# Latent attention: order of the query and key jobs between the score tiles, and the rope keys' split moved into the Fourier phase

## Chip, cores and metric

One NeuronCore of one Trainium2 chip runs the whole program. The metric is the device time of one execution in microseconds; the kernel before takes 3359.33 us (median of 3 runs, 3356.55 to 3360.12).

## The reference, cut to what matters

The program is a chain of two transformer blocks. The change lies in the first, which has two layers. Each layer projects 1040 tokens, mixes them by a Fourier transform, by average pooling and by a latent attention of four heads, gates and joins the three and multiplies by an output matrix. The attention is

```
def mla_mix(c_q, c_kv, k_r, q_norm_w, w_uq, kv_norm_w, w_ukv, cos, sin):
    dq = QK_NOPE_DIM + QK_ROPE_DIM                      # 128 + 64
    q = (rms_norm(c_q, q_norm_w) @ w_uq).reshape(B, L, MLA_HEADS, dq)
    q = concat([q[..., :QK_NOPE_DIM], apply_rope(q[..., QK_NOPE_DIM:], cos, sin)])
    kv = (rms_norm(c_kv, kv_norm_w) @ w_ukv).reshape(B, L, MLA_HEADS, QK_NOPE_DIM + V_HEAD_DIM)
    k_nope, v = kv[..., :QK_NOPE_DIM], kv[..., QK_NOPE_DIM:]
    k_rope = apply_rope(k_r, cos, sin)                  # one for all heads
    k = concat([k_nope, broadcast(k_rope)])
    s = einsum('bqhd,bkhd->bhqk', q, k) * dq ** -0.5
    return einsum('bhqk,bkhd->bqhd', softmax(s), v)
```

## The kernel before

All engines run one static program; `core.phase` opens a block with its own semaphores, and every engine passes from one block to the next. In each of the two layers the blocks are the input products, the Fourier and pool phase (`fourier_and_pool`, L864), and the heads together with the output product (`latent_heads`, L1068, inside `gemm`, L217).

**Precision.** Products that count run as sums of a high and a low part: a value x becomes x_hi (ACT, copied to the rounded type fp32r) and x_lo = x - x_hi (DVE). The projections of queries, keys and values (L1160, L1167) run in plain fp32, two matmul records for each 128-deep step.

**Fourier phase.** PE multiplies by a 64-point table (L909), then by the time tables (L922), each of the two channel halves j into four PSUM banks, then by the head matrices (L897). ACT evicts (L936, L942), DVE forms the spectrum from the evicted even part (L968, L972) and gates (L977). Between the pooling and the first spectrum, DVE applies the rotation to the keys (L957, L958, L960), for which it waits for the rope table, the last of the phase's DMAs (L891). PE's head product of half j waits for four DVE instructions of that half (L929).

**Heads.** The 1040 queries, padded to 1044, are 9 tiles of 116 rows (NH = 9, HT = 116), the keys and the query chunks 3 chunks of 348 columns (CH1). With four heads there are 36 score tiles, called steps s = 9n + i here: head n, step i. In step s PE does, in this order: `score(s)`, 15 matmuls into banks 0 to 2 (L1139); the jobs of the step (L1187); and nine transposes of the probabilities of step s - 1 into banks 3 to 5 (L1176). The next scores reuse banks 0 to 2 and wait for the exponential of step s (`exp_done`, L1130), and at i = 0, 3, 6 also for the query chunk i // 3 (L1128), at i = 0 for the head's keys (L1126). DVE takes in step s, in order: the row maximum (L1248) and its scaling (L1250), the rotation of a rope job (L1256, L1257, L1259), the reciprocal (L1262) and the normalisation (L1264), the low parts of the step's jobs (L1282) or the gated output of a value product (L1270), and the low part of the transposed tile s - 1 (L1293). ACT takes the exponential (L1201), the high parts of the jobs (L1211 to L1217) and of the transposed tile (L1234).

**Jobs.** `head_jobs` (L1040) is an order written by hand. There are five kinds: kn (a chunk of keys, 4 matmul records), qn and qr (a chunk of queries without and with rope, 6 records each), v (four tiles of values, 8 products) and pv (27 matmuls, probabilities times values for three tiles). All use PSUM banks 6 and 7 in turn: job j waits until job j - 2 is saved (L1147). pv also waits for the low part of its last transposed tile (L1151). Query chunks lie in two slots in turn (`slot_of`). The order before:

```
1044	    jobs = {0: [("qr", n, 1), ("qn", n, 1)], 1: [("pv", n - 1, 2)], 2: [("v", n, 0), ("v", n, 1)],
1045	            3: [("v", n, 2), ("qn", n, 2)], 4: [("pv", n, 0)], 5: [("qr", n, 2), ("kn", n + 1, 0)],
1046	            6: [("kn", n + 1, 1), ("kn", n + 1, 2)], 7: [("pv", n, 1)], 8: [("qr", n + 1, 0), ("qn", n + 1, 0)]}
```

Steps -4 to -1 hold only the jobs that step numbers of a head -1 would have; jobs of heads outside 0 to 3 fall away. SP loads the weights of heads 2 and 3 when the last query job of head n - 2 is done (L1115).

**Rope keys.** At the start of the heads ACT rounds the rotated keys twice, into both halves of `kr_hi` (L1195), and DVE forms `kr_lo` (L1241) and zeroes its second half (L1242). The first scores wait for it (L1123). While this goes on, POOL splits a weight tile of the output product (L199, L203).

**End.** In steps 33, 34, 36 and 37 ACT and DVE also split rows of the mixed result for the output product (`first_tile`, L324 and L330), whose first matmuls (L212) follow the last scores' exponential.

Of the kernel before, what the change touches and what calls it, by code (L numbers as in the profile page):

```python
# [822 lines left out]
def first_block(core, io, h, ident, ones):  # L823
# [6 lines left out]
    for layer in range(LAYERS):  # L830
        with core.scope():
# [4 lines left out]
            with core.scope():  # L836
# [11 lines left out]
                with core.scope():  # L848
                    fourier_and_pool(core, io, layer, slots, mix, r, vecs)
            with core.scope():  # L850
                heads = partial(latent_heads, core, io, layer, slots, mix, r, wqk, ident, HeadTensors(core))
# [12 lines left out]
def fourier_and_pool(core, io, layer, slots, mix, rope, vecs):  # L864
# [13 lines left out]
    first = (0, L1 - QT * NQ)  # L878

    with core.phase("z_done", "z_saved", *[f"tab{t}" for t in range(NQ)], "time_done", "even_saved", "spectrum_ready",  # L880
                    "pool_done", "pool_saved", "head_done", "rope_parts", "rope_in") as (block, *sems):
# [3 lines left out]
         rope_in) = sems[2 + NQ:]  # L885
# [46 lines left out]
        @block.scalar  # L932
        def _(act):
            for t in range(NQ):
                act.wait_ge(z_done, t + 1)
                nc.scalar.activation(z[:, t].rearrange("p j a n -> p (j a n)"), core.psum[0:QT, t % 2, :],  # L936
                                     ACT.Copy).then_inc(z_saved, 1)
            for j in range(2):
                act.wait_ge(time_done, j + 1)
                even = evens[:, j, :]  # L940
                for half in range(2):
                    nc.scalar.activation(even[:, half * HA:half * HA + widths[half]],  # L942
                                         core.psum[:, 4 * j + half, 0:widths[half]],
                                         ACT.Copy).then_inc(even_saved, 1)

        @block.vector
        def _(dve):
# [12 lines left out]
            nc.vector.tensor_tensor(kr, kr, krs, ALU.add)  # L960
# [79 lines left out]
def head_jobs(s):  # L1040


    n, i = divmod(s, NH)
    jobs = {0: [("qr", n, 1), ("qn", n, 1)], 1: [("pv", n - 1, 2)], 2: [("v", n, 0), ("v", n, 1)],
            3: [("v", n, 2), ("qn", n, 2)], 4: [("pv", n, 0)], 5: [("qr", n, 2), ("kn", n + 1, 0)],
            6: [("kn", n + 1, 1), ("kn", n + 1, 2)], 7: [("pv", n, 1)], 8: [("qr", n + 1, 0), ("qn", n + 1, 0)]}
    return [job for job in jobs[i] if 0 <= job[1] < MLA_HEADS]


class HeadTensors:  # L1050
# [3 lines left out]
    def __init__(self, core):  # L1054
        kn0 = core.sb("kn_hi", [P, TP], FR, 32), core.sb("kn_lo", [P, TP], FR, 32)
        self.kr_hi, self.kr_lo = core.sb("kr_hi", [P, TP], FR, 32), core.sb("kr_lo", [P, TP], FR, 32)
# [8 lines left out]
        self.qa, self.qb = (core.sb(name, [64, CH1], align=32) for name in ("rope_cos", "rope_sin"))  # L1065


def latent_heads(core, io, layer, slots, mix, rope, wqk, ident, tensors, first_tile):  # L1068
# [6 lines left out]
    steps = range(-4, tiles + 2)  # L1075
# [8 lines left out]
    kr = slots[0:64, KR, :]  # L1084
# [19 lines left out]
    with core.phase("kr_hi_done", "kr_lo_done", "pads_set", "wqk_in2", "wqk_in3", "job_done", "job_hi", "job_saved", "qr_step",  # L1104
                    "qr_ready", "scores_done", "max_ready", "bias_ready", "exp_done", "inv_done", "prob_ready",
                    "turned_done", "turned_hi", "turned_saved") as \
            (block, kr_hi_done, kr_lo_done, pads_set, wqk_in2, wqk_in3, job_done, job_hi, job_saved, qr_step, qr_ready,
# [5 lines left out]
        def _(sp):  # L1113
            for n in (2, 3):
                sp.wait_ge(job_done, number["qr", n - 2, 2] + 1)  # L1115
# [3 lines left out]
        def _(pe):  # L1119
            def score(s):  # L1120
                n, i = divmod(s, NH)
                if s == 0:
                    pe.wait_ge(kr_lo_done, 2)  # L1123
# [69 lines left out]
        def _(act):  # L1193
            for half in range(2):
                nc.scalar.activation(kr_hi[64 * half:64 * half + 64], kr, ACT.Copy).then_inc(kr_hi_done, 1)  # L1195
# [3002 lines left out]
```

## Time and profile before

| | |
|---|---|
| median of 3 runs | 3359.33 us (3356.55 to 3360.12) |
| the profiled execution, its own time | 3359.92 us |
| its span | 3358.1 us |
| PE busy | 3196.7 us, 95% |
| weight loads (PEld) busy | 2726.0 us, 81% |
| DVE busy | 2058.2 us, 61% |
| ACT busy | 1010.1 us, 30% |
| POOL busy | 938.9 us, 28% |

One slice of the page's 40 is 84 us; the heads of layer 0 are in slices 4 to 7, those of layer 1 in slices 11 to 14. PE shows 8 or 9 tenths busy in each. The time of the profiled execution is 1.8 us above its span, the part before and after the first and last instruction. In a timeline row the duration of a merged group of matmuls includes the modelled tail of its last; the distance to the start of the next group is the time that PE gave to it.

### The profile page before, as it was taken

Reading aid. Unit: us, or ns where it says so; the run is one execution under the profiler, and the core shown is the slowest. Engines: PE = TensorE matmul, PEld = TensorE weight load, DVE = VectorE, ACT = ScalarE, POOL = GpSimd, SP = SyncE. Lnnn points to the kernel's source line nnn. Section 1 sums busy time; section 2 is a strip of 40 time slices with the busy share of each in tenths; the row PEclk is TensorE's granted clock in tenths of the full one; section 3 lists DMA queues with packets and bytes.
Section 4 is the critical chain, followed back from the end, with each engine's and each line's share of the span. In section 5 each row is a group of like instructions: output and inputs, shape, how many; then the busy total and the mean of one; then the engine's idle time right before and its main releaser. Section 6 shows DMA issues by size and latency. Waiting matters only on the chain. (4 is left out here: it accounts for less than half of the span.)

```text
span 3358.1 us, 41800 instructions
## 1 busy us (share of the span) xinstructions
PE 3196.7 (95%) x17082; PEld 2726.0 (81%) x17082; DVE 2058.2 (61%) x2422; ACT 1010.1 (30%) x1456; POOL 938.9 (28%) x617
## 2 busy tenths in 40 slices
PE   8998999999899999999998999999999999999997
PEld 7997888999788898878867996666777787888875
DVE  5535664444466634556456554655676766897788
ACT  2113332101233320000022221555432644344643
POOL 3320001233000032333224322100142443555575
PEclk9999999999999999999999999999999999999998
DMA  3120000211100013323331003211361454455443
GB/s 135 45 65 9 21 1 20 77 45 45 33 21 8 1 45 135 130 93 97 103 126 54 1 1 111 72 42 38 117 227 59 146 172 156 132 183 171 147 158 119
DMA packets 111758, 282.12 MB, mean 84 GB/s; under 512 B 15010, under 2 KB 20770, under 8 KB 111552
## 3 DMA queue, kind: packets, MB, share of 16 engines
q1 hardware_dynamic: 107104, 263.19, 23.4%
q10 hardware_dynamic: 4464, 16.25, 1.2%
q8 instruction: 136, 2.23, 0.3%
q14 instruction: 54, 0.44, 0.0%
HBM read 237.37 MB, written 41.42 MB: 83 GB/s over the span
## 5 line engine op out<-in xcount | busy, mean ns | idle before, releaser
L3639 PE MATMUL psum<-x,w_hi 128*128 128x512 f32 x2016 | 627.0, 392 | 8.3 <-DVE x L3610 3.1
L199 POOL CAST w_hi<-w_raw 128x1024 fp32r<-128x1024 f32 x116 | 126.2, 1088 | 1795.9 <-PE psum L212 1112.0
L3639 PEld LDWEIGHTS psum<-x,w_hi 128*128 128x128 f32 x2016 | 379.1, 189 | 93.1 <-issue 6.9
L3639 PE MATMUL psum<-x,w_lo 128*128 128x512 f32 x1008 | 393.4, 390 | 0.0
L3524 POOL TENSOR_TENSOR w_lo<-w_sum,w_hi 128x512 fp32r<-128x512 f32 x180 | 252.9, 1412 | 330.0 <-ACT w_hi L3518 330.0
L727 PE MATMUL psum<-h,w_hi 128*128 128x512 f32 x1024 | 328.1, 402 | 15.2 <-PEq L126 11.5
L203 POOL TENSOR_TENSOR w_lo<-w_raw,w_hi 128x1024 fp32r<-128x1024 f32 x116 | 301.9, 2602 | 16.4 <-DVE y L1533 7.2
L727 PEld LDWEIGHTS psum<-h,w_hi 128*128 128x128 f32 x1024 | 190.2, 192 | 63.1 <-issue 21.9
L3639 PEld LDWEIGHTS psum<-x,w_lo 128*128 128x128 f32 x1008 | 190.0, 189 | 39.8
L212 PE MATMUL psum<-hn_hi,w_hi 128*128 128x348 f32 x864 | 188.9, 327 | 16.5 <-DVE hn_lo L409 15.1
L727 PE MATMUL psum<-h,w_lo 128*128 128x512 f32 x512 | 202.7, 396 | 0.0
L212 PE MATMUL psum<-h,w_hi 128*128 128x512 f32 x736 | 197.1, 389 | 0.0
L212 PE MATMUL psum<-hn_lo,w_hi 128*128 128x348 f32 x864 | 185.2, 323 | 0.0
L212 PE MATMUL psum<-hn_hi,w_lo 128*128 128x348 f32 x864 | 184.9, 322 | 0.0
L3518 ACT ACTIVATE w_hi<-w_sum 128x512 fp32r<-128x512 f32 x180 | 112.3, 630 | 208.2 <-DVE w_sum L3506 208.1
L212 PEld LDWEIGHTS psum<-hn_hi,w_hi 128*128 128x128 f32 x864 | 146.7, 189 | 20.2 <-issue 12.7
L212 PEld LDWEIGHTS psum<-h,w_hi 128*128 128x128 f32 x736 | 138.1, 188 | 28.7 <-issue 0.2
L1201 ACT ACTIVATE prob<-psum,softmax_small 116x1044 f32<-116x1044 f32 x72 | 81.5, 1132 | 227.2 <-DVE softmax_small L1250 227.2
L212 PEld LDWEIGHTS psum<-hn_lo,w_hi 128*128 128x128 f32 x864 | 147.2, 190 | 0.0
L212 PEld LDWEIGHTS psum<-hn_hi,w_lo 128*128 128x128 f32 x864 | 146.6, 189 | 0.0
L3506 DVE TENSOR_TENSOR w_sum<-w_raw 128x512 f32<-128x512 f32 x121 | 119.8, 993 | 28.5 <-PE psum L3639 22.2
L1167 PE MATMUL psum<-kept_slots,wqk 128*128 128x348 f32 x384 | 122.4, 466 | 11.0 <-DVE kn_lo L1282 7.8
(464 smaller groups left out, 6491.4 us busy)
## 6 DMA issues: line engine op xcount, KB each, us to landing
w_raw<-in_w_mlp SPq DMA_DIRECT2D x169, 256.0 KB, 2.9
norm_factor<-in_w_mlp SPq DMA_DIRECT2D x87, 256.0 KB, 2.8
w_raw<-in_w_mlp SPq DMA_DIRECT2D x42, 512.0 KB, 3.4
w_raw<-in_w_in SPq DMA_DIRECT2D x36, 512.0 KB, 3.4
w_raw<-in_w_gates SPq DMA_DIRECT2D x32, 512.0 KB, 4.2
gates_kept<-gate_stage SPq DMA_DIRECT2D x64, 256.0 KB, 2.1
gates<-gates_kept SPq DMA_DIRECT2D x32, 512.0 KB, 3.3
w_raw<-in_w_out SPq DMA_DIRECT2D x24, 512.0 KB, 3.5
```

Of the source, the lines that this page charges most:

```text
L199: self.core.nc.gpsimd.tensor_copy(self.hi[:, g % 2], self.raw[:, g % 2]).then_inc(self.hi_done, 1)
L203: self.core.nc.gpsimd.tensor_tensor(self.lo[:, g % 2], self.raw[:, g % 2], self.hi[:, g % 2].bitcast(F32), ALU.subtract) \
L212: last = nc.tensor.matmul(acc[:, c, :], w[:, g % 2, k, :], x(k)[:, c * ch:(c + 1) * ch], start=(k == 0 and part == 0), stop=(k == kt - 1 a ...
L727: last = nc.tensor.matmul(self.core.psum[:, self.bank(x // KT), :], one[:, g % 2, k, :], other(k)[:, c * CH2:(c + 1) * CH2], start=(k == 0 ...
L1167: last = nc.tensor.matmul(bank(j), wqk[n % 2][:, k0 + k, cols], slots[:, src + k, chunk(c)], start=(k == 0), stop=(k == kt - 1))
L1201: nc.scalar.activation(prob[s % 2].rearrange("p (c n) -> p c n", c=3), scores, ACT.Exp, bias=nmx[:, s % 2:s % 2 + 1], scale=MLA_SCALE, acc ...
L3506: self.core.nc.vector.tensor_tensor(self.slot(self.core.weights.sums, j), raw[:, 0:4], raw[:, 4:8], self.SUMS[q]).then_inc(self.w_summed, 1)
L3518: self.core.nc.scalar.activation(self.slot(self.core.weights.hi, j), self.weight_source(j), ACT.Copy) \
L3524: self.core.nc.gpsimd.tensor_tensor(self.slot(w.lo, j), self.weight_source(j), self.slot(w.hi, j).bitcast(F32), ALU.subtract).then_inc(sel ...
L3639: last = self.core.nc.tensor.matmul(out, one[:, k, :], other[:, k, :], start=(group == 0 and k == 0 and part == 0), stop=(group == second ...
```

## The change

The order of jobs is rewritten, so that a query chunk is made at least one step before the scores that need it; steps begin at -9 instead of -4, so that the jobs of a head -1 all run ahead. The split of the rope keys moves out of the heads into the Fourier phase, into which the heads' tensors are passed; for that, the heads' memory is laid out first and `kr_hi` and `kr_lo` stand at its end, beyond what the Fourier phase uses. The wait for head weights goes by qn instead of qr.

```diff
-                with core.scope():
-                    fourier_and_pool(core, io, layer, slots, mix, r, vecs)
             with core.scope():
-                heads = partial(latent_heads, core, io, layer, slots, mix, r, wqk, ident, HeadTensors(core))
+                tensors = HeadTensors(core)
+                heads = partial(latent_heads, core, io, layer, slots, mix, r, wqk, ident, tensors)
+            with core.scope():
+                core.sb("early_slots", [P, CKV + A_GATE - F_GATE, TP])
+                fourier_and_pool(core, io, layer, slots, mix, r, vecs, tensors)
...
         def _(act):
...
+            act.wait_ge(kr_ready, 1)
+            for half in range(2):
+                nc.scalar.activation(kr_hi[64 * half:64 * half + 64], slots[0:64, KR, :], ACT.Copy) \
+                    .then_inc(kr_hi_done, 1)
             for j in range(2):
                 act.wait_ge(time_done, j + 1)
...
-            nc.vector.tensor_tensor(kr, kr, krs, ALU.add)
+            nc.vector.tensor_tensor(kr, kr, krs, ALU.add).then_inc(kr_ready, 1)
+            dve.wait_ge(kr_ready, 1)
+            dve.wait_ge(kr_hi_done, 2)
+            nc.vector.tensor_tensor(kr_lo[0:64], kr, kr_hi[0:64].bitcast(F32), ALU.subtract)
+            nc.vector.tensor_tensor(kr_lo[64:P], kr_hi[64:P].bitcast(F32), kr_hi[64:P].bitcast(F32), ALU.subtract)
...
-    jobs = {0: [("qr", n, 1), ("qn", n, 1)], 1: [("pv", n - 1, 2)], 2: [("v", n, 0), ("v", n, 1)],
-            3: [("v", n, 2), ("qn", n, 2)], 4: [("pv", n, 0)], 5: [("qr", n, 2), ("kn", n + 1, 0)],
-            6: [("kn", n + 1, 1), ("kn", n + 1, 2)], 7: [("pv", n, 1)], 8: [("qr", n + 1, 0), ("qn", n + 1, 0)]}
+    jobs = {0: [("kn", n + 1, 0), ("kn", n + 1, 1)], 1: [("pv", n - 1, 2)], 2: [("v", n, 0), ("v", n, 1)],
+            3: [("v", n, 2), ("qr", n, 2)], 4: [("qn", n, 2), ("pv", n, 0)], 5: [("qr", n + 1, 0)],
+            6: [("qn", n + 1, 0)], 7: [("kn", n + 1, 2), ("pv", n, 1)], 8: [("qr", n + 1, 1), ("qn", n + 1, 1)]}
...
-    steps = range(-4, tiles + 2)
+    steps = range(-NH, tiles + 2)
...
-                sp.wait_ge(job_done, number["qr", n - 2, 2] + 1)
+                sp.wait_ge(job_done, number["qn", n - 2, 2] + 1)
...
-                    pe.wait_ge(kr_lo_done, 2)
...
-            for half in range(2):
-                nc.scalar.activation(kr_hi[64 * half:64 * half + 64], kr, ACT.Copy).then_inc(kr_hi_done, 1)
...
-            dve.wait_ge(kr_hi_done, 2)
-            nc.vector.tensor_tensor(kr_lo[0:64], kr, kr_hi[0:64].bitcast(F32), ALU.subtract).then_inc(kr_lo_done, 1)
-            nc.vector.tensor_tensor(kr_lo[64:P], kr_hi[64:P].bitcast(F32), kr_hi[64:P].bitcast(F32), ALU.subtract) \
-                .then_inc(kr_lo_done, 1)
```

## Rows read from the trace of the kernel before

**Rows 1.** Waits of PE, 235:545: engine, line, output, releaser: us in total, times, longest

```profile
PE psum L1139 <- DVE qr_both L1282: 5.4, 4, 2.2
PE psum L1139 <- DVE qn_lo L1282: 4.9, 4, 1.7
```

**Rows 2.** Timeline, start of layer 0's heads: start us, us, engine, line, operation

```profile
268.39 2.58 PE L1167 MATMUL psum<-kept_slots,wqk 128*128 128x348 f32 x8 [1.59 <-PEq L126]
...
269.55 2.35 POOL L203 TENSOR_TENSOR w_lo<-w_raw,w_hi 128x1024 fp32r<-128x1024 f32 x1
270.57 0.91 ACT L1215 ACTIVATE kn_hi<-psum 128x348 fp32r<-128x348 f32 x2
270.57 2.42 DVE L1241 TENSOR_TENSOR kr_lo<-kept_slots,kr_hi 64x1044 fp32r<-64x1044 f32 x1 [2.08 <-ACT kr_hi L1195]
...
274.87 6.56 PE L1167 MATMUL psum<-kept_slots,wqk 128*128 128x348 f32 x16 [3.90 <-DVE kn_lo L1282]
...
283.17 0.70 PE L1139 MATMUL psum<-kn_hi,qn_hi 128*116 128x348 f32 x3 [1.73 <-DVE qn_lo L1282]
```

**Rows 3.** Timeline of PE, head 1: scores' first group, value product, transposes

```profile
345.43 0.71 PE L1139 MATMUL psum<-kn_hi,qn_hi 128*116 128x348 f32 x3 [1.07 <-DVE qn_lo L1282]
...
354.90 0.40 PE L1155 MATMUL psum<-pT_hi,v_hi 116*128 116x348 f32 x1
...
359.26 1.05 PE L1176 MATMUL psum<-ident,prob 116*116 116x116 f32 x9
360.08 0.70 PE L1139 MATMUL psum<-kn_hi,qn_hi 128*116 128x348 f32 x3
...
372.29 0.70 PE L1139 MATMUL psum<-kn_hi,qn_hi 128*116 128x348 f32 x3
...
409.43 0.70 PE L1139 MATMUL psum<-kn_hi,qn_hi 128*116 128x348 f32 x3 [1.07 <-DVE qn_lo L1282]
```

**Rows 4.** Timeline of DVE and PE, head 0, step 1 to step 2

```profile
291.70 1.25 DVE L1248 TENSOR_REDUCE softmax_small<-psum 116x1 f32<-116x1044 f32 x1 [0.56 <-PE psum L1139]
...
294.44 0.73 PE L1139 MATMUL psum<-kn_hi,qn_hi 128*116 128x348 f32 x3 [1.88 <-ACT prob L1201]
```

**Rows 5.** Timeline, head 3, step 5 (one rope job) to step 6

```profile
508.31 0.70 PE L1139 MATMUL psum<-kn_hi,qn_hi 128*116 128x348 f32 x3
...
510.75 1.92 PE L1167 MATMUL psum<-kept_slots,wqk 128*128 128x348 f32 x6
...
512.51 1.06 PE L1176 MATMUL psum<-ident,prob 116*116 116x116 f32 x9
512.71 0.51 DVE L1256 TENSOR_TENSOR rope_cos<-psum,norm_factor 64x348 f32<-64x348 f32 x1 [0.32 <-PE psum L1167]
...
515.79 0.72 PE L1139 MATMUL psum<-kn_hi,qn_hi 128*116 128x348 f32 x3 [2.23 <-DVE qr_both L1282]
515.86 1.25 DVE L1293 TENSOR_TENSOR pT_lo<-psum,pT_hi 116x1044 fp32r<-116x1044 f32 x1
```

**Rows 6.** Timeline, head 3, steps 6 and 7 and the end

```profile
519.45 1.25 DVE L1248 TENSOR_REDUCE softmax_small<-psum 116x1 f32<-116x1044 f32 x1 [2.34 <-PE psum L1139]
...
526.79 0.40 PE L1155 MATMUL psum<-pT_hi,v_hi 116*128 116x348 f32 x1 [1.98 <-issue]
...
532.69 1.05 PE L1176 MATMUL psum<-ident,prob 116*116 116x116 f32 x9
...
539.53 0.75 PE L212 MATMUL psum<-mix_hi,w_hi 128*128 128x348 f32 x3 [1.43 <-ACT prob L1201]
```

**Rows 7.** Windows of 1 us: length, PE, PEld, DVE, ACT, POOL, then PEclk, DMA

```profile
296.00:297.00 1.00, 1.00 (x5) 1.00 (x4) 0.60 (x1) 0.00 (x0) 0.00 (x0) 0.50 0.00 0
...
528.00:529.00 1.00, 1.00 (x5) 1.00 (x4) 0.03 (x1) 0.93 (x1) 0.00 (x0) 0.50 0.00 0
```

**Rows 8.** Timeline, Fourier phase of layer 0

```profile
250.93 1.24 DVE L960 TENSOR_TENSOR kept_slots<-kept_slots,mix 64x1044 f32<-64x1044 f32 x1
...
262.40 1.92 PE L897 MATMUL psum<-early_slots,last 128*128 128x348 f32 x6
```

More of the change, by code:

```diff
@@ L861, in first_block, with fourier_and_pool @@
     return vecs, r[:], comes_first
-def fourier_and_pool(core, io, layer, slots, mix, rope, vecs):
+def fourier_and_pool(core, io, layer, slots, mix, rope, vecs, tensors):
     nc = core.nc
@@ L878, in fourier_and_pool @@
     first = (0, L1 - QT * NQ)
+    kr_hi, kr_lo = tensors.kr_hi, tensors.kr_lo
     with core.phase("z_done", "z_saved", *[f"tab{t}" for t in range(NQ)], "time_done", "even_saved", "spectrum_ready",
-                    "pool_done", "pool_saved", "head_done", "rope_parts", "rope_in") as (block, *sems):
+                    "pool_done", "pool_saved", "head_done", "rope_parts", "rope_in", "kr_ready",
+                    "kr_hi_done") as (block, *sems):
         z_done, z_saved = sems[0:2]
@@ L884, in fourier_and_pool @@
         (time_done, even_saved, spectrum_ready, pool_done, pool_saved, head_done, rope_parts,
-         rope_in) = sems[2 + NQ:]
+         rope_in, kr_ready, kr_hi_done) = sems[2 + NQ:]
         @block.sync
@@ L1055, in __init__ @@
         kn0 = core.sb("kn_hi", [P, TP], FR, 32), core.sb("kn_lo", [P, TP], FR, 32)
-        self.kr_hi, self.kr_lo = core.sb("kr_hi", [P, TP], FR, 32), core.sb("kr_lo", [P, TP], FR, 32)
         kn1 = core.sb("kn_hi", [P, TP], FR, 32), core.sb("kn_lo", [P, TP], FR, 32)
@@ L1065, in __init__ @@
         self.qa, self.qb = (core.sb(name, [64, CH1], align=32) for name in ("rope_cos", "rope_sin"))
+        self.kr_hi, self.kr_lo = core.sb("kr_hi", [P, TP], FR, 32), core.sb("kr_lo", [P, TP], FR, 32)
 def latent_heads(core, io, layer, slots, mix, rope, wqk, ident, tensors, first_tile):
@@ L1083, in latent_heads @@
     small, prob, kn_hi, kn_lo, kr_hi, kr_lo, qa, qb = t.small, t.prob, t.kn_hi, t.kn_lo, t.kr_hi, t.kr_lo, t.qa, t.qb
-    kr = slots[0:64, KR, :]
     scores = core.psum[0:HT, 0:3, 0:CH1]
@@ L1103, in v_bank @@
         return core.psum[0:HT, 6 + j % 2, 0:n * P].rearrange("p (t n) -> p t n", t=n)
-    with core.phase("kr_hi_done", "kr_lo_done", "pads_set", "wqk_in2", "wqk_in3", "job_done", "job_hi", "job_saved", "qr_step",
+    with core.phase("pads_set", "wqk_in2", "wqk_in3", "job_done", "job_hi", "job_saved", "qr_step",
                     "qr_ready", "scores_done", "max_ready", "bias_ready", "exp_done", "inv_done", "prob_ready",
                     "turned_done", "turned_hi", "turned_saved") as \
-            (block, kr_hi_done, kr_lo_done, pads_set, wqk_in2, wqk_in3, job_done, job_hi, job_saved, qr_step, qr_ready,
+            (block, pads_set, wqk_in2, wqk_in3, job_done, job_hi, job_saved, qr_step, qr_ready,
              scores_done, max_ready, bias_ready, exp_done, inv_done, prob_ready, turned_done, turned_hi,
```

## The prediction

> **What bounds the kernel now.** I read the page first: PE is busy in 95% of the span (the table above), no other engine above 61%. So the change can gain only PE's idle time and time at the lower clock. Then the waits of PE over the heads of layer 0. Two of them are for a query chunk made one step before it is used, 5.4 and 4.9 us, four times each [rows 1]. Then the timeline of PE with its distances from start to start, and around each wait the other engines. Layer 1 repeats layer 0, so I work out one layer and double it.
>
> **Prices on PE**, all start to start. Scores 2.44, from 508.31 to 510.75; a q job 1.76 [rows 5]. Transposes 0.82; pv 4.36 [rows 3], of which I keep 4.30 where another job stands before it. A kn is 1.17: the row of eight records is 2.58 long with a tail of 0.24 [rows 2]. A step is thus 3.26 plus its jobs. But the next scores also wait for the exponential. DVE starts 0.20 after PE hands over (the rope multiply at 512.71 after the job that ends at 512.51 [rows 5]), and from the start of the maximum to the next scores it is 2.74 (291.70 to 294.44 [rows 4]). So no step is under 2.44 + 0.20 + 2.74 = 5.38.
>
> **The start.** Now: two kn, then PE stands 3.90, since the rope keys' low part, 2.42 on DVE, is ahead of kn's on DVE; then sixteen records take 6.56, and scores begin at 283.17, 14.78 after 268.39 [rows 2]. After: kn0 is out at 269.6; its rounding (half of the 0.91 for two [rows 2]) and its low part (0.5, as the rope multiply of the same 348 columns [rows 5]), with handovers, let qr0 start at 270.9; qn0 follows. kn2 must wait until qr0 is saved. The multiply starts 1.96 after its job's start, at 272.9, and in head 3 the scores waited for the same saving until 3.08 after the multiply [rows 5]; here the reciprocal and scaling are not between, so I take 2.9. kn2 starts at 275.8, after a stall of 1.3, and with kn2, qr1 and qn1 (4.69) scores start at 280.45. Gain 2.7, with two more q jobs already done. Their 3.5 us come back as shorter later steps.
>
> **Head 0.** Step 0: two kn, 2.44 + 2.34 is under the floor: 5.38. Step 1: no job, 5.38. Steps 2 and 3 keep their jobs' sum; they take 12.21 in head 1 [rows 3]. In head 0 the clock falls in step 2, after the stall of 1.88 [rows 4]: the granted clock of one of its stretches is 0.50, 1.2 instead of 2.4 GHz [rows 7]. I count 1.6 for it before and after. Step 4: qn and pv, 2.44 + 1.76 + 4.30 + 0.82 = 9.32. Step 5: one qr, 3.26 + 1.76 = 5.02, so the floor holds, 5.38.
>
> Step 6 is where the change gives something back. In a step with a lone qr, DVE's last low part starts 3.15 after the multiply and takes 1.25 [rows 5], so it ends 4.40 + 3.15 + 1.25 = 8.80 after the step's scores began. The next scores began at 5.38 and their maximum could start at 8.02; it starts at 8.84. Step 6 lasts 8.84 + 2.74 - 5.38 = 6.20, against 5.02 of work. Step 7: kn and pv, 8.73. Step 8: two q jobs, 6.78, without today's wait of 1.07. Steps 4 to 8 give 36.41. Head 0 is 5.38 + 5.38 + 12.21 + 1.6 + 36.41 = 60.98, before 62.26 (283.17 to 345.43): **1.3 gained**.
>
> **Heads 1 and 2.** Before 64.00 (345.43 to 409.43), and nearly the same in head 2. Now steps 4 to 8 take 37.14 (372.29 to 409.43), steps 0 and 1 14.65 (345.43 to 360.08) [rows 3]. After: step 0 is 3.26 + 2.34 = 5.60. The pv of step 1 waits for DVE's last instruction of step 0, which two kn low parts make later: 2.64 + 2.74 + 0.9 (reciprocal and scaling, an estimate: under the 1.25 of a low part of equal length) + 1.05 (two low parts of a chunk) + 1.25 = 8.6 after step 0 began, 0.65 after pv could start; today it is 0.25. Step 1: 3.26 + 4.36 + 0.65 = 8.27. The sum is 13.87 + 12.21 + 36.41 = 62.49: **1.5 gained in each**. In step 3 the qr moves behind v and its saving is late, so step 4's maximum is some 1.3 late; pv covers that.
>
> **Head 3.** No head follows, so steps 0, 5, 6 and 8 have no jobs. After: 5.38; 3.26 + 4.36 = 7.62; 12.21; 9.32; 5.38; then step 6 starts. In it DVE and ACT also split rows for the output product, and pv of step 7 starts 7.34 after step 6's maximum (519.45 to 526.79). That keeps, so pv starts 2.64 + 7.34 = 9.98 after step 6 began. pv 4.36, and from the transposes behind it to the output product 6.84 (532.69 to 539.53) [rows 6]. Sum 61.1. Before: 539.53 - 473.4 = 66.1, with 473.4 as 409.43 + 64.0. **5.0 gained**, half of it the lower clock before, in step 6 and in the pv (526.79 to 532.69 is 5.90 for 4.36 [rows 6]; a stretch in it was granted 0.50 [rows 7]).
>
> **The clock.** Before, three of the stalls of 1.88 or more were followed by the lower clock: 1.88 [rows 4], 2.23 [rows 5], the one of 1.98 before the pv [rows 6]; that of 1.06 to 1.07 (row 409.43) was not. After, head 3 has empty steps 0, 5 and 6, each with a stall of 2.1, and one of 2.2 before the last pv but one. If each lowers the clock, 1.6 + 1.0 + 1.5 come back (one falls inside the wait of pv). The shortest of them is at the edge of what the rows show, so I take 2.7 of 4.1. Ends: 0 and 4.1.
>
> **The Fourier phase.** The key rotation ends at 252.2. ACT rounds twice, 2.2, until 254.4, and evicts even part 0 some 0.7 later than now; DVE then runs both low parts, 2.42 + 1.24 at most, until 258.1, and four spectrum instructions, until 259.5. PE does not need them before 262.40 [rows 8]. I count zero; the cover is 2.9 of time products. Without it the price would be at most those 2.2 + 3.7 = 5.9 a layer. The 2.42 is long because POOL runs a subtract from 269.55 to 271.90 while DVE, of the same length otherwise as the 1.24 of the rotation [rows 8], begins at 270.57 [rows 2]: DVE starts its work only when POOL is done. The Trainium skill, page "SBUF — State Buffer", section "SBUF: two separate sides", has the rule: a DVE instruction with two SBUF inputs and a GpSimd instruction that reads SBUF exclude each other, each for its whole length. By it the low part would take 1.24 in the Fourier phase, where POOL is idle, and the cover would be 4.1; the sum stays.
>
> **SP, memory.** The weights of heads 2 and 3 are asked for one step earlier and needed four steps earlier, still over four steps after the request. Addresses change for the heads' tensors only; no row prices that, zero, between -1 and +1 a layer.
>
> **Sum per layer:** 2.7 + 1.3 + 3.0 + 5.0 - 2.7 = 9.3; two layers 18.6. The profiled execution took 3359.9, 0.6 above the median: 3341.3 in its terms, 3340.7 against the median. I say 3341.
>
> **Rivals.**
> **A, lower clock nearly gone** (12%): none of head 3's stalls lowers it, and head 0's step 2 keeps the full clock too. 12.0 + 1.6 a layer: 3332. For it: none of the stalls below 1.1 did so. Against: that of 1.88 did.
> **B, the heads become DVE's** (8%): the late maxima of steps 4, 6 and 1 don't heal, since DVE starts each next step late. Then each head loses some 2 more, 8 a layer, and about 1 a layer is left: 3357, no change. Against it: after every pv DVE has over 4 us to catch up.
> **C, slower by the clock** (3%): every stall over a microsecond, some twelve a layer, costs one lowering of 1.5, 18 a layer. It decides from eight on: 12.0 - 18 is 6 a layer lost, 3371. Against it: the stalls of 1.06 and 1.07 in the rows, followed by full speed.
> **D, the rope split on the path** (4%): head products wait for the spectrum, up to 5.9 a layer, 3.4 are left: 3353, no change that can be told. Against it: the cover of 2.9.
> My own case: 73%.
>
> **Range.** 3332 to 3349: the low end is A, the high end all of head 3's lowered clocks and 0.07 us of error on each of 72 steps. About 0.2%, 6.7 us, is what a measurement of this kernel can tell from no change. Faster by more: my case and A, 0.85; within: B and D, 0.12; slower: C, 0.03.
>
> **What would show it.** PE's waits for qr_both and qn_lo in scores gone; in their place waits for the exponential, about 0.4 in step 5 and 1.2 in step 6 of heads 0 to 2 and 2.1 in the empty steps of head 3. First scores 12.1 after the heads' first matmul. No wait of PE in the Fourier phase beyond today's; the rope low part at 1.24 there. A longer distance from step 6 to step 7, or waits of pv over 0.7, would make B right; PEclk under 1 in heads 1 and 2, C. The step that I trust least is the clock in head 3.

## The result, and the profile after

| | before | after |
|---|---|---|
| median | 3358.01 us (3356.55 to 3360.12, 4 runs) | 3337.27 us (3336.07 to 3342.22, 4 runs) |
| profiled execution | 3359.92 us | 3342.22 us |
| its span | 3358.1 us | 3340.4 us |

Both kernels ran side by side on one chip. The ratio is 0.994 with a 95% interval of 0.9924 to 0.9955: 20.7 us less. The forecast was 3341, so 3.7 too high, and inside its range.

From the page of the changed kernel (busy us of each engine, share of the span, instructions):

```profile
PE 3194.2 (96%) x17082; PEld 2724.5 (82%) x17082; DVE 2054.5 (62%) x2422; ACT 1010.0 (30%) x1456; POOL 939.5 (28%) x617
```

PE does the same work in 17.7 us less span. The waits of PE in the heads of layer 0 (line, releaser: us in total, times, longest), to be held against [rows 1]:

```profile
PE psum L1149 <- ACT prob L1209: 10.3, 11, 1.9
...
PE psum L1165 <- issue: 2.4, 3, 2.0
...
PE psum L1177 <- DVE qr_both L1286: 1.1, 1, 1.1
...
PE psum L901 <- DVE early_slots L984: 0.5, 1, 0.5
```

The scores (now L1149) no longer wait for a query chunk. They wait for the exponential only. The start of the heads, in the timeline of all engines (start, us, engine, line), the rows that answer to [rows 2, 4 and 8]:

```profile
253.34 1.24 DVE L971 TENSOR_TENSOR kr_lo<-kept_slots,kr_hi 64x1044 fp32r<-64x1044 f32 x1 [2.31 <-ACT kr_hi L944]
...
258.56 0.42 DVE L984 TENSOR_TENSOR early_slots<-even_part,psum 128x259 f32<-128x259 f32 x1
...
265.46 1.92 PE L901 MATMUL psum<-early_slots,last 128*128 128x348 f32 x6
...
271.46 6.29 PE L1177 MATMUL psum<-kept_slots,wqk 128*128 128x348 f32 x20 [1.59 <-PEq L126]
...
276.03 0.51 DVE L1260 TENSOR_TENSOR rope_cos<-psum,norm_factor 64x348 f32<-64x348 f32 x1 [0.94 <-PE psum L1177]
...
278.84 4.95 PE L1177 MATMUL psum<-kept_slots,wqk 128*128 128x348 f32 x16 [1.09 <-DVE qr_both L1286]
...
283.36 0.90 PE L1149 MATMUL psum<-kn_hi,qn_hi 128*116 128x348 f32 x3
...
294.35 0.73 PE L1149 MATMUL psum<-kn_hi,qn_hi 128*116 128x348 f32 x3 [1.88 <-ACT prob L1209]
```

The rope keys' low part is made at 253.34, in 1.24 us instead of 2.42. Twenty records of the first jobs run on end, and the scores start at 283.36, 11.90 after 271.46. Head 1, steps 6 and 7, DVE and PE, to be held against [rows 5]:

```profile
383.56 0.70 PE L1149 MATMUL psum<-kn_hi,qn_hi 128*116 128x348 f32 x3 [0.22 <-ACT prob L1209]
...
385.64 1.25 DVE L1297 TENSOR_TENSOR pT_lo<-psum,pT_hi 116x1044 fp32r<-116x1044 f32 x1
...
386.80 1.24 DVE L1252 TENSOR_REDUCE softmax_small<-psum 116x1 f32<-116x1044 f32 x1
...
389.54 0.72 PE L1149 MATMUL psum<-kn_hi,qn_hi 128*116 128x348 f32 x3 [0.73 <-ACT prob L1209]
...
398.29 0.71 PE L1149 MATMUL psum<-kn_hi,qn_hi 128*116 128x348 f32 x3
```

The maximum at 386.80 stands behind the low part at 385.64, and step 6 lasts 5.98. Head 3, the scores of steps 6 and 7, the value product, and the output product (answers to [rows 6]):

```profile
507.28 0.70 PE L1149 MATMUL psum<-kn_hi,qn_hi 128*116 128x348 f32 x3 [1.65 <-ACT prob L1209]
...
512.66 0.73 PE L1149 MATMUL psum<-kn_hi,qn_hi 128*116 128x348 f32 x3 [1.89 <-ACT prob L1209]
...
517.26 0.40 PE L1165 MATMUL psum<-pT_hi,v_hi 116*128 116x348 f32 x1 [1.98 <-issue]
...
523.16 1.05 PE L1186 MATMUL psum<-ident,prob 116*116 116x116 f32 x9
...
529.99 0.74 PE L212 MATMUL psum<-mix_hi,w_hi 128*128 128x348 f32 x3 [1.43 <-ACT prob L1209]
```

The value product from 517.26 to 523.16 takes 5.90 for 4.36. It is a lowered stretch, a piece of PE's work at the lower clock: a microsecond of it (length, PE, PEld, DVE, ACT, POOL, PEclk, DMA, GB/s) was granted half the clock, 1.2 instead of 2.4 GHz, as one before in [rows 7]:

```profile
519.00:520.00 1.00, 1.00 (x5) 1.00 (x5) 0.18 (x2) 1.00 (x3) 0.00 (x0) 0.50 0.00 0
```

Step by step, from one scores' start to the next, in layer 0:

| us | forecast | measured |
|---|---|---|
| first matmul of the heads to first scores | 12.06 | 11.90 |
| head 0, step 0; step 1 | 5.38; 5.38 | 5.57; 5.42 |
| head 0, steps 2 and 3 | 12.21 + 1.6 | 12.26, at the full clock |
| heads 1 and 2, steps 0 and 1 | 13.87 | 13.63 (head 1) |
| steps 2 and 3 of head 1 | 12.21 | 12.22 |
| step 4 of head 1 | 9.32 | 9.32 |
| step 5; step 6 | 5.38; 6.20 | 5.47; 5.98 |
| step 7; step 8 | 8.73; 6.78 | 8.75; 6.78 |
| head 0; 1; 2 | 60.98; 62.49; 62.49 | 59.56; 62.15; 62.21 |
| head 3 | 61.1, and 2.7 of clock | 62.71, of which 1.54 clock |

Layer 1 gives the same lengths within 0.03, but for two: step 2 of its head 0 takes 8.35 instead of 6.80, at the lower clock, and its head 3 keeps the full clock. **Where the time came from:** from the heads' first matmul to the output product's first it was 271.14 and 271.15 us in the two layers, and is 258.53 and 258.60. That is 25.2 less. Part of it is clock. Before, each layer had four lowered stretches in its heads: the sixteen records behind the stall of 3.90 [rows 2], which take 6.56 where sixteen take 4.95 at 278.84 after the change, step 2 of head 0 (8.34 for 6.80), and steps 6 and 7 of head 3 (6.40 and 11.32, for 5.42 and 9.80 in the split-only kernel below). The window around the first of them, before:

```profile
275.00:281.00 6.00, 6.00 (x16) 3.74 (x16) 1.98 (x5) 0.46 (x1) 0.00 (x0) 0.74 0.00 0
```

Together the four cost 5.7 a layer and the one left after costs 1.5, so about 4.1 of the 12.6 a layer is the lower clock, and the rest is waits. The span is 17.7 shorter, so 7.5 went elsewhere. 3.1 of it lie ahead of the heads of layer 0: their first matmul starts at 271.46 instead of 268.39 [rows 2]. Nearly all of the rest, 4.2, lies behind them: from the first output product to the end it is 2204.95 instead of 2200.76. What these are is taken up below.

### The profile page after: what moved, and what is told of

It reads as the page before. It is cut to its first block and busy times, and to the rows that moved or that the text cites. A ratio compares the mean times of both kernels' runs of the same rounds, so it can differ in the third digit from the quotient of the medians.

```text
span 3340.4 us, 41800 instructions
## 1 busy us (share of the span) xinstructions
PE 3194.2 (96%) x17082; PEld 2724.5 (82%) x17082; DVE 2054.5 (62%) x2422; ACT 1010.0 (30%) x1456; POOL 939.5 (28%) x617
## 5 line engine op out<-in xcount | busy, mean ns | idle before, releaser
L727 PE MATMUL psum<-h,w_hi 128*128 128x512 f32 x1024 | 328.8, 403 | 15.2 <-PEq L126 11.5
```

The source lines that it names most:

```text
L727: last = nc.tensor.matmul(self.core.psum[:, self.bank(x // KT), :], one[:, g % 2, k, :], other(k)[:, c * CH2:(c + 1) * CH2], start=(k == 0 ...
```

## Experiments

Ten runs. Each ran beside the kernel before on its chip; the difference in us is against the median of those runs. The first four ran on one chip, the next three on another, the last three on a third.

**Splitting the change.** First the rope split alone, with the old order of jobs.

```diff
-    steps = range(-NH, tiles + 2)
+    steps = range(-4, tiles + 2)
...
+    jobs = {0: [("qr", n, 1), ("qn", n, 1)], 1: [("pv", n - 1, 2)], 2: [("v", n, 0), ("v", n, 1)],
+            3: [("v", n, 2), ("qn", n, 2)], 4: [("pv", n, 0)], 5: [("qr", n, 2), ("kn", n + 1, 0)],
+            6: [("kn", n + 1, 1), ("kn", n + 1, 2)], 7: [("pv", n, 1)], 8: [("qr", n + 1, 0), ("qn", n + 1, 0)]}
...
-                sp.wait_ge(job_done, number["qn", n - 2, 2] + 1)
+                sp.wait_ge(job_done, number["qr", n - 2, 2] + 1)
```

> The change with the old order of jobs and steps from -4: only the rope keys' split is in the Fourier phase. My theory (two parts that add up: the split frees the start of the heads, the order frees the chunk waits): scores of layer 0 begin about 9.1 us after the heads' first matmul instead of 14.8, no lowered clock there, all later steps as before with the 1.0 to 1.3 us waits for qr_both and qn_lo; 5.7 a layer, some 11 us under before (about 3347). Rival one (the split alone is the gain, the order is given back as DVE lateness): the full 20 us, about 3338. Rival two (the order alone is the gain): as before, 3358.

Measured: 3345.11 (3343.16 to 3346.94) against 3359.99, ratio 0.9957 (0.9942 to 0.9972), 14.9 less. Its waits of PE in layer 0's heads:

```profile
PE psum L1149 <- DVE qr_both L1286: 5.4, 4, 2.2
PE psum L1149 <- DVE qn_lo L1286: 5.0, 4, 1.7
PE psum L1149 <- ACT prob L1209: 3.8, 2, 1.9
```

The first jobs and the first scores in its timeline:

```profile
270.71 7.46 PE L1177 MATMUL psum<-kept_slots,wqk 128*128 128x348 f32 x24 [1.58 <-PEq L126]
...
279.90 0.71 PE L1149 MATMUL psum<-kn_hi,qn_hi 128*116 128x348 f32 x3 [1.73 <-DVE qn_lo L1286]
```

With the split away, the three kn, the qr and the qn run as one row of 24 records, and the scores start 9.19 after the first of them instead of 14.78: 5.6 a layer, 11.2 in all. The two waits for query chunks stand as in [rows 1]. The median fell by 14.9 where some 11 were expected; a part of the rest is clock: the heads of layer 1 took 265.84, 5.3 less than before; those of layer 0 263.08, 8.1 less, though the program is the same: in their head 3 steps 6 and 7 ran at the full clock, 5.42 and 9.80, and in layer 1's at the lower, 6.66 and 11.31. Both rivals are refuted: the gain is neither 20 nor nothing.

Then the order alone, with the rope split where it was.

```diff
-    steps = range(-4, tiles + 2)
+    steps = range(-NH, tiles + 2)
...
+    jobs = {0: [("kn", n + 1, 0), ("kn", n + 1, 1)], 1: [("pv", n - 1, 2)], 2: [("v", n, 0), ("v", n, 1)],
+            3: [("v", n, 2), ("qr", n, 2)], 4: [("qn", n, 2), ("pv", n, 0)], 5: [("qr", n + 1, 0)],
+            6: [("qn", n + 1, 0)], 7: [("kn", n + 1, 2), ("pv", n, 1)], 8: [("qr", n + 1, 1), ("qn", n + 1, 1)]}
```

> The new order of jobs, with the rope keys' split still at the start of the heads. My theory: PE again stands about 3.9 us after two kn jobs and then runs for a while at the lower clock; the first scores begin some 17 to 18 us after the first matmul (two more query jobs ahead of them than before), 5 to 6 later than in the full change; the steps afterwards as in the full change. 6 to 7 us a layer under before, about 3345. The low part of the rope keys again 2.42 us beside POOL's subtract. Rival one (split alone): 3358. Rival two (order alone): 3338.

Measured: 3348.33 (3345.07 to 3349.52) against 3359.99, ratio 0.9965 (0.995 to 0.9979), 11.7 less. The timeline at the start of layer 0's heads:

```profile
273.48 2.35 POOL L203 TENSOR_TENSOR w_lo<-w_raw,w_hi 128x1024 fp32r<-128x1024 f32 x1
...
274.51 2.42 DVE L1241 TENSOR_TENSOR kr_lo<-kept_slots,kr_hi 64x1044 fp32r<-64x1044 f32 x1 [2.08 <-ACT kr_hi L1195]
...
278.81 3.78 PE L1167 MATMUL psum<-kept_slots,wqk 128*128 128x348 f32 x12 [3.90 <-DVE kn_lo L1282]
```

The timeline of PE at the same place in layer 1:

```profile
887.87 5.44 PE L1167 MATMUL psum<-kept_slots,wqk 128*128 128x348 f32 x12 [3.90 <-DVE kn_lo L1282]
```

Windows inside the jobs that follow the stall, in layer 0 and in layer 1 (columns as above):

```profile
279.00:283.00 4.00, 3.58 (x12) 2.00 (x11) 1.72 (x4) 0.42 (x2) 0.00 (x0) 1.00 0.00 0
889.00:893.00 4.00, 4.00 (x11) 2.30 (x9) 1.35 (x3) 0.00 (x0) 0.00 (x0) 0.72 0.00 0
```

The step lengths are those of the full change, lowered stretches apart (steps 6 and 7 of head 3 take 6.93 and 9.78 in layer 0, 5.40 and 11.34 in layer 1); what is missing is the start. The heads took 262.33 and 263.99, 8.8 and 7.2 less than before where 6 to 7 were expected, because layer 0 kept the full clock behind the stall; the median, 3348, is still 3 above the expected 3345, and the first product of the Fourier phase, taken up below, was 3.0 longer here than before. So the two parts add up to more than the whole: 14.9 and 11.7 against 20.7. They overlap at the start: with the split still in the heads, the new order's first scores come 15.86 after the first matmul, one microsecond later than before, so on top of the new order the split is worth 15.86 - 11.90 = 4.0 a layer, not 5.6. 11.7 and 2 x 4.0 are 19.7 of the 20.7. The pair also shows two things to be used below. POOL's subtract ends at 275.83, and DVE's low part, begun at 274.51, takes 2.42 as in [rows 2]. And the same stall of 3.90, in the same place of the same program, is followed by the full clock in layer 0 (twelve records in 3.78) and by the lower one in layer 1 (5.44, granted 0.72 over four us).

**Step 6, where the change gives something back.** Its cause in the forecast was the qr of step 5, whose low part goes ahead of the transposed tile's on DVE and is late. Exchanging the two q jobs should take that away:

```diff
-            3: [("v", n, 2), ("qr", n, 2)], 4: [("qn", n, 2), ("pv", n, 0)], 5: [("qr", n + 1, 0)],
-            6: [("qn", n + 1, 0)], 7: [("kn", n + 1, 2), ("pv", n, 1)], 8: [("qr", n + 1, 1), ("qn", n + 1, 1)]}
+            3: [("v", n, 2), ("qr", n, 2)], 4: [("qn", n, 2), ("pv", n, 0)], 5: [("qn", n + 1, 0)],
+            6: [("qr", n + 1, 0)], 7: [("kn", n + 1, 2), ("pv", n, 1)], 8: [("qr", n + 1, 1), ("qn", n + 1, 1)]}
```

> The full change with step 5 and step 6 exchanged: qn in step 5, qr in step 6. My theory (in step 6 PE waits 0.7 beyond the softmax floor of 5.38 because the rope job of step 5 makes DVE's last low part, and so the next maximum, late): step 5 5.4 to 5.5 and step 6 5.4 to 5.5 instead of 5.98, step 7 as now, since its kn job covers the late pv; 0.5 to 0.6 us in each of heads 0 to 2, 3 to 4 us in all, about 3334. Rival (step 6 is set by PE or ACT, not by DVE's lateness): step 6 stays at 5.98, no gain.

Measured: 3333.55 (3330.65 to 3338.24) against 3359.99, ratio 0.9924 (0.9909 to 0.9939). Head 1, step 6, in its timeline:

```profile
381.86 0.71 PE L1149 MATMUL psum<-kn_hi,qn_hi 128*116 128x348 f32 x3 [0.22 <-ACT prob L1209]
...
383.05 1.23 DVE L1297 TENSOR_TENSOR pT_lo<-psum,pT_hi 116x1044 fp32r<-116x1044 f32 x1
...
384.51 1.25 DVE L1252 TENSOR_REDUCE softmax_small<-psum 116x1 f32<-116x1044 f32 x1 [0.22 <-PE psum L1149]
...
387.25 0.76 PE L1149 MATMUL psum<-kn_hi,qn_hi 128*116 128x348 f32 x3
```

The low part starts at 383.05, 1.19 after the step's scores instead of 2.08 (383.56 to 385.64), and the maximum at 384.51 waits for PE only. Step 6 is 5.39 (381.86 to 387.25) instead of 5.98, step 7 8.78 instead of 8.75. The wait for the exponential falls from 10.3 to 8.1 us. That cause is shown. It is worth 0.6 in each of three heads, 1.8 a layer. The exchange also touches the start, where qn now stands ahead of qr: PE waits 1.7 for the rope job instead of 1.1, and 0.6 is given back. The heads took 257.37 and 257.40, 1.2 a layer less than under the change, one lowered stretch in each as there. The medians differ by 3.7 (3337.27 to 3333.55), against their own neighbours by 5.7; of that the edit explains 2.4. In the profiles 3.0 more is the Fourier phase's clock, below; the medians' remainder is not shown to come from it.

**Fuller steps.** In the change, steps 0, 5 and 6 have little work and stand at the floor of the exponential, while step 7 has a kn beside its pv and step 8 two q jobs. This order moves one kn into each of the light steps:

```diff
+    jobs = {0: [("qr", n, 1), ("kn", n + 1, 0)], 1: [("pv", n - 1, 2)], 2: [("v", n, 0), ("v", n, 1)],
+            3: [("v", n, 2), ("qr", n, 2)], 4: [("qn", n, 2), ("pv", n, 0)], 5: [("qr", n + 1, 0), ("kn", n + 1, 1)],
+            6: [("qn", n + 1, 0), ("kn", n + 1, 2)], 7: [("pv", n, 1)], 8: [("qn", n + 1, 1)]}
```

> The full change with the jobs spread so that steps 0, 5 and 6 each hold a q and a kn job, step 7 only pv, step 8 only qn: 0 qr(n,1), kn(n+1,0); 5 qr(n+1,0), kn(n+1,1); 6 qn(n+1,0), kn(n+1,2); 7 pv(n,1); 8 qn(n+1,1). My theory (a step costs the larger of 3.26 plus its jobs and the softmax floor of 5.38, and pv adds what DVE's low part is late): steps 5 and 6 6.2 each, step 7 about 8.0 with a wait of 0.4 before pv, step 8 5.4, step 0 6.2; first scores 10.9 after the first matmul instead of 11.9; about 2.3 us a layer under the full change, 3333. Rival (PE is never short of work in steps 5 to 8, the sum of jobs decides): no difference beyond the first scores.

Measured: 3328.36 (3325.95 to 3331.32) against 3359.99, ratio 0.9907 (0.9893 to 0.9922). Its start:

```profile
270.46 4.33 PE L1177 MATMUL psum<-kept_slots,wqk 128*128 128x348 f32 x14 [1.58 <-PEq L126]
...
276.47 5.15 PE L1177 MATMUL psum<-kept_slots,wqk 128*128 128x348 f32 x16 [1.67 <-DVE qr_both L1286]
...
281.19 0.90 PE L1149 MATMUL psum<-kn_hi,qn_hi 128*116 128x348 f32 x3
```

Its wait for the exponential, layer 0's heads:

```profile
PE psum L1149 <- ACT prob L1209: 6.1, 6, 1.9
```

Scores start 10.73 after the first job. Steps 5 and 6 are 6.2 each, steps 7 and 8 7.9 and 5.5. PE's wait for the exponential is 6.1 instead of 10.3, and the heads took 254.90 and 256.45 instead of 258.5; the longer of the two has a lowered stretch in head 3, the other none. By step lengths the order saves 2.1 a layer, for 2.3 expected: 1.17 at the start, 1.21 in head 0, 0.43 in each of heads 1 and 2, and 1.15 lost in head 3, whose step 1 takes 8.72 for 7.56. So the rival by which only the start would gain is refuted. But the median is 9 below the change's where these lengths make 4.2; the repetition takes that up.

**Head 3, step 7.** The last value product but one waits 2 us after its scores ([rows 6], 517.26 after) because ACT and DVE split rows for the output product ahead of the transposed tile. Here the first two pieces are split two steps earlier.

```diff
-                if s in (tiles - 3, tiles - 2):
-                    first_tile.vector(dve, range(2 * (s - tiles) + 6, 2 * (s - tiles) + 8))
+                if s in (tiles - 5, tiles - 2):
+                    first_tile.vector(dve, range(0, 2) if s == tiles - 5 else range(2, 4))
```

The same for ACT.

> The full change with the first two row splits for the output product taken from step 6 of head 3 to its step 4, the next two stay in step 7. My theory (step 7 of head 3 takes 9.8 to 11.3 because the splits of step 6 make DVE's low part late, for which pv waits 2.0 to 2.2): step 7 of head 3 takes 7.6, step 4 stays at 9.3 since its pv covers 2.4 us more of DVE; 2.2 us a layer, more where the clock had been lowered in that pv; about 3332. Rival (that pv waits for something else, or step 4 has no room on DVE): step 7 keeps its length, or steps 5 and 6 grow by what step 7 loses; 3337.

Measured: 3335.03 (3333.45 to 3339.09) against 3359.06, ratio 0.9926 (0.9911 to 0.9942). The timeline of head 3, end of step 4 to step 5:

```profile
501.39 2.39 DVE L330 TENSOR_TENSOR mix_lo<-mix,mix_hi 128x1044 fp32r<-128x1044 f32 x2
...
503.70 1.24 DVE L1297 TENSOR_TENSOR pT_lo<-psum,pT_hi 116x1044 fp32r<-116x1044 f32 x1
504.86 1.24 DVE L1252 TENSOR_REDUCE softmax_small<-psum 116x1 f32<-116x1044 f32 x1
...
505.09 1.08 PE L1186 MATMUL psum<-ident,prob 116*116 116x116 f32 x9 [0.91 <-DVE pT_lo L1297]
...
507.68 1.04 PE L1149 MATMUL psum<-kn_hi,qn_hi 128*116 128x348 f32 x3 [1.51 <-ACT prob L1209]
```

The stall before the value product is gone, and step 7 is 7.58 instead of 9.78 (layer 1, full clock). But the split of 2.39 now stands ahead of the low part at 503.70, for which the transposes of step 5 wait 0.91, and step 5 is 6.10 instead of 5.48. Layer 1's heads took 257.02 instead of 258.60: net 1.6 of the 2.2, so part of the gain comes back as a new wait. That is in part the rival's case. Layer 0's heads took 258.58, no less than under the change, since steps 6 and 7 of head 3 were both lowered there (6.94 and 9.13). The median is 2.2 below the change's, where 5 were expected; against the kernel before beside it, it is 24.0 less instead of 20.7.

> The jobs spread as before (steps 0, 5 and 6 a q and a kn job each) together with the row splits in step 4 of head 3. If both reasons hold, the gains add: some 4.5 to 5 us under the spread order, 3323 to 3324. Rival (the empty steps of head 3 just hand the time on to the next step): 3328.

That is the edit of the one before on the spread order. Measured: 3328.09 (3323.95 to 3329.73) against 3359.06, ratio 0.9902 (0.9887 to 0.9917). 31.0 less than the kernel before beside it, where the spread order alone had 31.6: no gain that can be told from this pair. In layer 1 the heads took 253.34, in layer 0, with a lowered stretch in head 3, 254.86; without it the step lengths are 1.6 a layer below the spread order's.

**The cover of the Fourier phase.** The forecast counted the moved split at zero because the spectrum has time to spare; the cover is the time by which DVE may be later before PE waits. Two reciprocals, whose results nothing uses, are put behind the split on DVE to take 10.0 us.

```diff
             nc.vector.tensor_tensor(kr_lo[64:P], kr_hi[64:P].bitcast(F32), kr_hi[64:P].bitcast(F32), ALU.subtract)
+            nc.vector.reciprocal(mix[:, 4, 0:L1], slots[:, CQ, 0:L1])
+            nc.vector.reciprocal(mix[:, 5, 0:L1 // 2], slots[:, CQ, 0:L1 // 2])
```

> The full change with two reciprocals more on DVE behind the rope keys' low parts in the Fourier phase, of 1040 and 520 columns, about 6.7 and 3.3 us, into rows of the mixed result that nobody reads before they are written anew. My theory (the split is free there because PE needs the spectrum only after the second half's time products; cover 3.8 us in full clock, more where the clock is lowered at the start of the phase): the cover is used up and PE waits 2 to 6.5 us a layer before the first spectrum head product; 4 to 13 us over the full change, about 3345. Rival (DVE is free all through this phase): no change, 3337; other rival (no cover, the split costs already now): 20 us over it.

Measured: 3347.56 (3344.79 to 3350.21) against 3359.06, ratio 0.9965 (0.995 to 0.9981). Its timeline in the Fourier phase of layer 0:

```profile
257.39 6.65 DVE L973 RECIPROCAL mix<-kept_slots 128x1040 f32<-128x1040 f32 x1
...
263.96 3.35 DVE L974 RECIPROCAL mix<-kept_slots 128x520 f32<-128x520 f32 x1
...
268.65 5.81 PE L901 MATMUL psum<-early_slots,last 128*128 128x348 f32 x12 [5.39 <-DVE early_slots L986]
```

10.0 us more on DVE made PE wait 5.4 in layer 0 and 5.9 in layer 1, where the change has 0.5 for its own second half. The twelve records behind that wait then ran at the lower clock, 5.81 in layer 0 and 5.69 in layer 1, where the twelve at the start of this phase took 3.75 at the full clock. Their window in layer 0:

```profile
268.60:274.50 5.90, 5.81 (x12) 3.28 (x12) 2.58 (x6) 0.00 (x0) 0.00 (x0) 0.65 0.00 0
```

The waits are 5.4 + 5.9 - 2 x 0.5 = 10.3 more than in the change, and the lower clock behind them is 4.0 more. The gain over the kernel before shrinks only from 20.7 to 11.5, by 9.2; in the profiles 4.7 come back because the twelve records at the start of the phase took 3.75 in both layers here and 6.77 and 5.44 in the change. The cover is 10.0 - 5.4 = 4.6 in layer 0 and 4.1 in layer 1, both times with those records at the full clock. The split in the change stays inside it: in layer 0 its last spectrum instruction ends at 258.98 and PE takes up the head product at 265.46. Both rivals, no change and 20 us over, are refuted.

**The repetition.** The change, the spread order and the spread order with early rows again, together on one chip, because the first three had run on different ones.

> The change as it is, once more. My theory (order and waits are fixed, what varies is where PE's clock is lowered): every unlowered step of the heads as long as in the first profile to 0.05 us; lowered stretches in other places; 3337, some 20 to 21 under before. Rival (the difference between forecast and first result lies in the steps): step lengths change with it.

> The spread order once more, beside the change on one chip. By the step lengths of its first profile it is 0.9 us a layer shorter at the start, 0.6 in head 0, 0.6 in each of heads 1 and 2 and longer by 0.9 in step 1 of head 3; with equal clock 4 to 6 us under the change. If its first result of 9 us under the change was the clock's, 3331 to 3333; if the fuller steps also keep the clock up, again 3328.

> The spread order with the two row splits in step 4 of head 3, beside both. By the step lengths 1.6 us a layer under the spread order (step 7 2.2 shorter, step 5 0.6 longer): 3 us under it. Rival (nothing is left of it, since the time goes to the next stall): equal to the spread order.

Measured, against 3358.62: the change 3337.8 (3336.79 to 3338.03), ratio 0.9934 (0.9922 to 0.9947); the spread order 3328.56 (3326.97 to 3331.5), ratio 0.9908 (0.9895 to 0.9922); with early rows 3327.27 (3324.14 to 3330.45), ratio 0.9901 (0.9884 to 0.9918). The order of the three is as expected; early rows bring 1.3 where 3 was expected, within what the runs spread, so their gain is shown in the heads' lengths and not in the time. From the heads' first matmul to the output product the three take 258.55 and 258.56; 254.91 and 254.91; 253.28 and 253.34. The unlowered steps of the change came again within 0.05, as expected. Its lowered stretches were expected in other places and stood in the same two: step 7 of head 3 in layer 0 (11.33) and step 2 of head 0 in layer 1 (8.35).

Between the change and the spread order the medians differ by 9.2, the case of fuller steps that also keep the clock up, and not that of equal clock. Step lengths explain 2.1 a layer of it, 4.2 (the expectation had put them at 1.8 a layer, with 0.6 in head 0 for 1.2): the change's heads without their one lowered stretch would be 257.0. Those stretches, absent in this profile of the spread order (its first had one), are 3.0. The remaining 2.0 are not placed: outside the heads the spread order's profile is 0.8 longer than the change's (2819.9 and 2819.1), and its execution (3331.5) is the slowest of its four. **The best version found** is the spread order, with or without early rows: 3327 to 3329, some 9 below the change and 30 below the kernel before.

## Why the prediction was right or wrong

**Removed waits.** Right. The waits of 5.4 and 4.9 us for query chunks [rows 1] are gone with the order (absent in the change and in the order-only kernel, present in the split-only kernel).

**The start.** Right: 11.90 for 12.06. From the saved multiply (276.03) to kn2 (278.84) it is 2.81 for the 2.9 taken, and the stall is 1.09 for 1.3. The split-only kernel shows what is inside: the moved split alone is worth 5.6 a layer, of which the new order gives 2.7 back for two more q jobs, and takes them out of later steps. Of the 5.6, some 1.6 is clock, the sixteen records that take 6.56 before.

**The floor of a step.** 5.38 was right to 0.1, 5.42 and 5.38 to 5.48 in the steps without a job; only step 0 of head 0, with two kn, had 5.57.

**Step 6.** The mechanism was right, and shown by the exchange of qr and qn. The size was 5.98 for 6.20. The forecast put the maximum 3.46 behind the step's scores (8.84 - 5.38), it came at 3.24 (383.56 to 386.80), and its chain to the next scores is 2.74 as taken (386.80 to 389.54). Of the 0.22, 0.13 is that the maximum begins 1.16 behind the start of the low part (385.64 to 386.80), where the forecast had 1.29 (8.84 less 8.80 - 1.25 = 7.55); the other 0.09 is that the step before was 5.47 and not 5.38, so that its late low part, 7.55 behind that step's scores as forecast, fell earlier in this one.

**Heads 1 and 2.** Right, 62.15 and 62.21 for 62.49. In head 1 steps 0 and 1 are 0.24 shorter than forecast (the pv of step 1 is less late) and step 6 0.22; step 5 is 0.09 longer.

**Head 3.** Right without the clock: 62.71 - 1.54 = 61.17 for 61.1. The pv's start, forecast 9.98 after step 6 began, came at 517.26 - 507.28 = 9.98.

**The clock: the term that was mis-sized.** The forecast counted 2.7 a layer in head 3 and 1.6 in step 2 of head 0, 4.3 together, since "three of the stalls of 1.88 or more were followed by the lower clock". Measured were 1.55: the value product of head 3 in layer 0, and step 2 of head 0 in layer 1 (8.35 for 6.80). The stalls themselves came nearly as forecast (in head 3 scores wait 1.59, 1.65 and 1.89 behind an empty step, for 2.1, of which the tail of the transposes takes 0.24; and 1.98 for 2.2 ahead of the pv), most of them with the full clock behind. The forecast's list was also short by one: the stall of 3.90 was followed by the lower clock too, granted 0.74 in the window shown above, and its 1.6 went unnamed into the start's gain. The heads shrank by 12.6 a layer and not by 9.3; of the difference of 3.3, this term is 2.75, heads 1 and 2 are 0.6, the start 0.2, heads 0 and 3 -0.25.

Step 2 of head 0 shows best why a length of stall is no measure. The stall ahead of it is 1.88 or 1.89 in all twelve profiles, in both layers. With the old order of jobs (before, split-only) the step took 8.34 to 8.37 in 4 of 4 layers; with the new order (the change twice, order-only, qn first, early rows, cover) 8.33 to 8.37 in 7 of 12 layers and 6.78 to 6.82 in 5; with the spread order (four profiles) 6.80 to 6.82 in 8 of 8. So the same stall can lower the clock or not.

**Outside the heads.** The forecast counted zero here. The first product of the Fourier phase, the head matrices on the pooling's rows (L897 before, L901 after), is a row of twelve records behind a wait of 2.75 in all twelve profiles, and it lies ahead of any changed instruction. The window around it before:

```profile
236.00:246.00 10.00, 9.31 (x58) 7.66 (x58) 2.61 (x2) 2.99 (x5) 0.00 (x0) 1.00 0.92 230
```

The same window after:

```profile
236.00:246.00 10.00, 10.00 (x45) 7.31 (x45) 2.61 (x2) 1.79 (x3) 0.00 (x0) 0.71 0.91 258
```

It took 3.75 before and 6.77 after, at a granted clock of 0.71: the 3.1 us named above. In the other profiles it took 3.75 in three (qn first, cover, spread again), 5.44 in three (split-only, spread, spread with early rows again) and 6.7 to 6.8 in four (order-only, early rows, spread with early rows, the change again). The same program, the spread order, gave 5.44 and 3.75, and order-only, which up to there is the kernel before, 6.74 for its 3.75, so the edit is not what decides. In layer 1 the same row took 5.19 before and 5.44 after, and over all twelve profiles 3.75 in two, 5.1 to 5.4 in nine and 6.78 in one. The 4.2 behind the heads did not come back: in the repetition the same stretch takes 2200.25, as before (2200.76), and over the twelve profiles it lies between 2196.3 and 2205.0. What makes it differ is open. All that lies outside the heads took 2813.4 to 2823.3 in eleven profiles, that of the reciprocals left aside.

So the forecast came out only 3.7 too high because two misses oppose each other. The heads shrank by 25.2 where 18.6 was forecast, 6.6 more; the medians differ by 20.7 only, so by the medians 4.5 were given back outside (7.5 by this pair of profiles, 3.3 by the profile of the repetition). That the two nearly cancel is luck: what lies outside the heads was counted at zero. The last 1.6 are bookkeeping: the sum was made from a profiled execution of 3359.9 and rounded down by 0.3, while the median of before beside the change is 3358.0.

**The Fourier phase.** Right. No wait of PE beyond the 0.5 of today. The cover was put at 2.9, or 4.1 if the low part takes 1.24; it takes 1.24 (253.34), and the cover measures 4.6 and 4.1, with the first product at the full clock. The rule of the Trainium skill, page "SBUF — State Buffer", section "SBUF: two separate sides", by which a DVE instruction with two SBUF inputs and a GpSimd instruction that reads SBUF exclude each other, gives that 1.24. The trace agrees: the same low part takes 2.42 beside POOL's subtract (before and order-only) and 1.24 where POOL is idle (the change).

**SP, memory.** Zero was right as far as the heads show it: no wait of theirs names the weights.

**Rivals.** A, the lower clock nearly gone, 3332: the heads went its way, with one lowered stretch a layer left, and the median fell between its time and that of the forecast's own case. B, heads bound by DVE: refuted, the late maxima heal behind each pv (step 7 took 8.75 for 8.73). C, slower by the clock: refuted, one lowering a layer; and of the twelve stalls over a microsecond that it counted, each layer of the heads has six, with 1.6 and 1.4 more at its two ends. D, the rope split on the path: refuted by the missing wait, and the cover kernel shows what D would have looked like.

## What to carry to other kernels

Once no job is late, the chain maximum, exponential, next scores is the floor of a light step (5.38 here for 3.3 of work), and what is left to gain lies in how evenly the jobs are spread: the same jobs in another order took off 9 us more than the change, 4 by step lengths and 3 by lowered stretches that its profile did not have. On the engine that finishes a step's results, count what stands ahead of the instruction that starts that chain; one exchange of two jobs was worth 0.6 us a head. Price what a stall does to the clock as a chance, from several executions, and not as a sum, and compare the stretches that the edit doesn't touch before the whole difference is put down to the edit: here they differ by up to 10 us from profile to profile.

## What was not expected of the hardware

The same stall in the same program does not always have the same consequence for TensorE's clock. The 3.90 us of the order-only kernel were followed by the full clock in one layer and by the lower one in the other; the 1.88 us before step 2 of head 0 by the lower one in 11 of 24 layers. A lowered stretch of the heads costs 1.0 to 1.7 us, the one at the start of the Fourier phase 1.4 to 1.7 or 3.0. At step 2 of head 0 the spread order had none in 8 layers, against 11 in 16 for the others. Fuller steps alone don't explain it: steps 1 and 2 hold the same jobs in all orders, and in step 0 the spread order has 2.93 of jobs, the change's order 2.34, lowered in 7 of 12, but the old order 3.52, lowered in 4 of 4. The cause is open.

A DVE instruction can begin before the recorded end of the one ahead of it: the maximum begins 1.16 behind the start of a low part of 1.25 (385.64 and 386.80).
